# Hybrid diffusion step: the experts' shift added after the gather, router products in column tiles, last turns moved between dense products

## What is computed

```
h2 = rms(x, p['g_ffn']) * (1 + sc2) + sh2
aff = jax.nn.softmax((h @ w_router).astype(jnp.float32), axis=-1)
gate, idx = lax.top_k(jnp.swapaxes(aff, 1, 2), cap)
xg = jax.vmap(lambda hb, ib: hb[ib])(h, idx)
a = jnp.einsum('becd,edf->becf', xg, w_e1)
g3 = jnp.einsum('becd,edf->becf', xg, w_e3)
y = jnp.einsum('becf,efd->becd', jax.nn.silu(a) * g3, w_e2) * gate[..., None].astype(h.dtype)
```

## Time and profile before

| | us |
|---|---|
| median of 3 runs (3504.83 to 3505.77) | 3505.09 |
| the profiled execution | 3505.53 |
| its span | 3503.7 |
| PE busy | 3288.9 (94%) |
| DVE busy | 2107.6 (60%) |
| ACT busy | 1409.9 (40%) |
| POOL busy | 363.4 (10%) |

### The profile page before, as it was taken

The page is one execution under the profiler, slowest core; times in us unless marked ns, Lnnn a source line. Parts: engine busy times, 40 slices in busy tenths (PEclk is TensorE's granted clock), DMA queues, the critical chain, the costliest instruction groups (busy, mean ns, idle before and its releaser), DMA issues. The chain is left out here.

```text
span 3503.7 us, 39989 instructions
## 1 busy us (share of the span) xinstructions
PE 3288.9 (94%) x16088; PEld 2554.8 (73%) x16088; DVE 2107.6 (60%) x1830; ACT 1409.9 (40%) x1295; POOL 363.4 (10%) x429
## 2 busy tenths in 40 slices
PE   6889999999998899997999999939999999999995
PEld 4678878888886899986888888725666666666663
DVE  3336555555553677763232243257888888888886
ACT  3122212221211444442121222236777777777774
POOL 0020010010100000000011111030112111111102
PEclk8999999999999999999999999969999999999997
DMA  9465545465542211106253444168999999999996
GB/s 376 179 171 201 186 169 190 152 236 190 203 172 91 82 37 42 36 22 258 103 192 132 144 165 147 58 253 309 377 396 380 388 398 387 385 397 396 384 404 230
DMA packets 142462, 790.13 MB, mean 226 GB/s; under 512 B 18992, under 2 KB 30288, under 8 KB 61408
## 3 DMA queue, kind: packets, MB, share of 16 engines
q1 hardware_dynamic: 101680, 668.72, 49.6%
q0 software_dynamic: 40656, 119.60, 11.2%
HBM read 720.39 MB, written 67.86 MB: 225 GB/s over the span
## 5 line engine op out<-in xcount | busy, mean ns | idle before, releaser
L99 DVE TENSOR_TENSOR w_lo<-w_stage,w_hi 128x2048 fp32r<-128x2048 f32 x384 | 880.1, 2296 | 141.9 <-ACT w_hi L94 141.9
L94 ACT ACTIVATE w_hi<-w_stage 128x2048 fp32r<-128x2048 f32 x384 | 736.8, 1920 | 307.6 <-PE e_ps L106 307.5
L104 PE MATMUL i_ps<-w_hi,hT_hi 128*128 128x512 f32 (+1 forms) x1440 | 568.5, 395 | 25.0 <-DVE hT_lo L561 12.9
L105 PE MATMUL i_ps<-w_lo,hT_hi 128*128 128x512 f32 (+1 forms) x1440 | 559.2, 388 | 0.0
L106 PE MATMUL i_ps<-w_hi,hT_lo 128*128 128x512 f32 (+1 forms) x1440 | 558.9, 388 | 0.0
L104 PE MATMUL e_ps<-w_hi,xgT_hi 128*80 128x512 f32 x1024 | 404.3, 395 | 2.5 <-DVE xgT_lo L2038 2.3
L105 PE MATMUL e_ps<-w_lo,xgT_hi 128*80 128x512 f32 x1024 | 404.0, 395 | 0.0
L106 PE MATMUL e_ps<-w_hi,xgT_lo 128*80 128x512 f32 x1024 | 401.6, 392 | 0.0
L104 PE MATMUL p_ps<-w_hi,xT_hi 128*128 128x512 f32 x960 | 378.6, 394 | 17.8 <-DVE xT_lo L1534 17.8
L106 PE MATMUL p_ps<-w_hi,xT_lo 128*128 128x512 f32 x960 | 374.9, 391 | 0.0
L105 PE MATMUL p_ps<-w_lo,xT_hi 128*128 128x512 f32 x960 | 374.6, 390 | 0.0
(11 more groups left out here) (322 smaller groups left out, 4438.2 us busy)
## 6 DMA issues: line engine op xcount, KB each, us to landing
w_stage<-in_w_e SPq DMA_DIRECT2D x384, 1024.0 KB, 8.5
w_stage<-in_w_ada SPq DMA_DIRECT2D x96, 1024.0 KB, 6.4
w_raw<-in_w_in SPq DMA_DIRECT2D x64, 1024.0 KB, 4.8
w_stage<-in_w_o_gm SPq DMA_DIRECT2D x16, 1024.0 KB, 7.5
w_stage<-in_w_o_mla SPq DMA_DIRECT2D x16, 1024.0 KB, 5.1
w_stage<-in_w_out SPq DMA_DIRECT2D x16, 1024.0 KB, 4.8
acts<-evacuated POOLq DMA_DIRECT2D x60, 256.0 KB, 4.4
side<-acts POOLq DMA_DIRECT2D x40, 256.0 KB, 5.5
```

Of the source, the lines that this page charges most:

```text
L94: act.activation(dst, src, ACT.Copy).then_inc(st.hi, 1)
L99: dve.tensor_tensor(dst, src, hi.bitcast(F32), ALU.subtract).then_inc(st.split, 1)
L104: pe.matmul(out, x_hi, w_hi, start=first, stop=False)
L105: pe.matmul(out, x_hi, w_lo, start=False, stop=False)
```

## The change

1. The router's weights lie in `M.c_st` (16 tiles of 32 columns, 16 of them written anew). Each of the four products of `route` goes to a column tile of its own (output partitions 32j to 32j+31, each with start and stop), so `logitT` has 128 partitions, and the four parts are added only in the router: `logitT` is turned in five 128x128 tiles, and two reductions add the four groups.
2. The last chunk's turns 0 to 2 and products 0 and 1 stand between and behind the last dense tiles of the last piece.
3. POOL no longer waits for the stores of `xn` at the end of the phase; SP waits for them before the eighth piece of experts' weights, and POOL before the first gather.
4. The rows go to `h2` scaled, without the shift, from 5 buffers. The shift is loaded as 32 rows of 128, turned on PE, and laid out by DVE as `shiftT` (128x16x80). DVE adds it to the turned rows (`rows_sum`, three more instructions per expert, reading PSUM, writing `x_sum`), ACT rounds from `x_sum`, DVE subtracts from `x_sum`.
5. In the loop ACT rounds the thirds at steps 17 and 21 (16 and 20 before). DVE adds at steps 16 and 20, and subtracts at steps 18 and 22 (16 and 20 before).
6. `load_x(0)` stands ahead of the last gather.

The diff, cut to what the text speaks of:

```diff
-    w_r = m.new("w_router_sb", [P, KT, EXPERTS], F32)
+    w_r = M.c_st
...
-    M.logitT = m.new("logitT", [EXPERTS, N_TOK], F32)
+    M.logitT = m.new("logitT", [P, N_TOK], F32)
...
+        M.xn_stored = stored
...
-                    sp.dma_start(w_r[:], I["w_router"][0].rearrange("(k p) n -> p k n", p=P)).then_inc(w_r_in, 16)
+                    sp.dma_start(w_r[:, :, 0:EXPERTS], I["w_router"][0].rearrange("(k p) n -> p k n", p=P)).then_inc(w_r_in, 16)
...
-            for t in range(TT):
-                pool.wait_ge(stored[t], 16 * 2 * N_CH)
...
-                for a, b, src in ((0, P, ps[6][0:EXPERTS, 0:P]), (P, N_TOK, ps[7][0:EXPERTS, :])):
+                for a, b, src in ((0, P, ps[6][:, 0:P]), (P, N_TOK, ps[7][:])):
...
-                out = ps[7][0:EXPERTS, bass.ts(t - 1, P)] if t else ps[6][0:EXPERTS, 0:P]
+                out = ps[7][:, bass.ts(t - 1, P)] if t else ps[6][:, 0:P]
                 for j in range(KG):
-                    ins = pe.matmul(out, w_r[:, KG * i + j, :], x[:, j, :], start=(j == 0), stop=(j == KG - 1))
+                    ins = pe.matmul(out[32 * j:32 * j + 32, :], w_r[:, KG * i + j, :], x[:, j, :], start=True, stop=True, skip_group_check=True)
                 ins.then_inc(logit, 1)
...
+                    if n == N_PIECES - 1 and t >= 2:
+                        turn_xg(N_CH - 1, t - 2)
+                        if t >= 3:
+                            route(N_CH - 1, t - 3)
                 if c == chunk(OUT, 0) and g == 3:
                     sum_shift()
-            for t in range(TT):
+            for t in (3, 4):
                 turn_xg(N_CH - 1, t)
-                if t:
-                    route(N_CH - 1, t - 1)
+                route(N_CH - 1, t - 1)
             route(N_CH - 1, TT - 1)
...
-    h_row = [m.new(f"h_row{b}", [P, D], F32) for b in range(3)]
-    shift = m.new("shift2_rows", [P, 2, D], F32)
+    h_row = [m.new(f"h_row{t}", [P, D], F32) for t in range(TT)]
...
+    x_sum = m.new("x_sum", [P, KT, SLOTS], F32)
...
+    shiftT = m.new("shift2T", [P, KT, SLOTS], F32)
+    shift_rows = m.new("shift2_rows", [2 * KT, P], F32)
+    shift_cols = m.new("shift2_by_tile", [P, 2, KT], F32)
...
+        h_out = M.pool_sem("r_h_out")
...
-                sp.dma_start(shift[:, r, :], M.mod[r:r + 1, 3 * D:4 * D].to_broadcast((P, D))).then_inc(shift_in, 16)
+                sp.dma_start(shift_rows[bass.ts(r, KT), :], M.mod[r, 3 * D:4 * D].rearrange("(k p) -> k p", p=P)).then_inc(shift_in, 16)
             for q in range(PB):
+                if q == PB - 1:
+                    for t in range(TT):
+                        sp.wait_ge(M.xn_stored[t], 16 * 2 * (D // NC))
                 load(q, q, E13[0][0, q])
...
-            pool.wait_ge(shift_in, 32)
             for t in range(TT):
                 pool.wait_ge(scaled, 4 * t + 4)
-                pool.tensor_tensor(h_row[t % 3][:], h_row[t % 3][:], shift[:, min(t, 1), :], ALU.add).then_inc(h_ok, 1)
-                pool.wait_ge(h_ok, t + 1)
-                pool.dma_start(M.h2[bass.ts(t, P), :], h_row[t % 3][:]).then_inc(h_out[t % 3], 16)
-            for b in range(3):
-                pool.wait_ge(h_out[b], 32 if b < 2 else 16)
+                pool.dma_start(M.h2[bass.ts(t, P), :], h_row[t][:]).then_inc(h_out, 16)
+            for t in range(TT):
+                pool.wait_ge(M.xn_stored[t], 16 * 2 * (D // NC))
+            pool.wait_ge(h_out, 16 * TT)
             pool.wait_ge(pick_ok, 2)
             gather(0)
             gather(1)
...
+            load_x(0)
...
-            for t in range(N_F):
+            for t in range(1, N_F):
                 load_x(t)
...
             def rows_hi(e, g):
-                act.wait_ge(x_tr, 3 * e + g + 4)
-                dst, src = turned_rows(e, g, True)
-                act.activation(dst, src, ACT.Copy).then_inc(x_hi, 1)
+                act.wait_ge(x_ok, 3 * e + g + 1)
+                a, b = TXG[g]
+                act.activation(xT_hi[:, a:b, :], x_sum[:, a:b, :], ACT.Copy).then_inc(x_hi, 1)
...
-                    if j == 16 and rows:
+                    if j == 17 and rows:
                         rows_hi(i + 2, 0)
                         rows_hi(i + 2, 1)
-                    if j == 20 and rows:
+                    if j == 21 and rows:
                         rows_hi(i + 2, 2)
 
             def scale_rows(t):
-                if t >= 3:
-                    act.wait_ge(h_out[t % 3], 16)
                 for i in range(4):
-                    act.activation(h_row[t % 3][:, bass.ts(i, NC)].rearrange("p (j n) -> p j n", j=KG), M.xg[i][t], ACT.Copy,
+                    act.activation(h_row[t][:, bass.ts(i, NC)].rearrange("p (j n) -> p j n", j=KG), M.xg[i][t], ACT.Copy,
                                    scale=st[:, 3, t:t + 1]).then_inc(scaled, 1)
 
...
+            def rows_sum(e, g):
+                if g == 0 and not (isinstance(e, int) and e == 0):
+                    dve.wait_ge(x_lo, 3 * e)
+                dve.wait_ge(x_tr, 3 * e + g + 4)
+                a, b = TXG[g]
+                dve.tensor_tensor(x_sum[:, a:b, :], pair[0][:, g % 2, 0:(b - a) * SLOTS].rearrange("p (k n) -> p k n", n=SLOTS),
+                                  shiftT[:, a:b, :], ALU.add).then_inc(x_ok, 1)
+
             def rows_lo(e, g):
                 dve.wait_ge(x_hi, 3 * e + g + 1)
-                dst, src = turned_rows(e, g, False)
-                sub(dst, src, turned_rows(e, g, True)[0]).then_inc(x_lo, 1)
+                a, b = TXG[g]
+                sub(xT_lo[:, a:b, :], x_sum[:, a:b, :], xT_hi[:, a:b, :]).then_inc(x_lo, 1)
...
                     if j == 16 and rows:
+                        rows_sum(i + 2, 0)
+                        rows_sum(i + 2, 1)
+                    if j == 18 and rows:
                         rows_lo(i + 2, 0)
                         rows_lo(i + 2, 1)
                     if j == 19:
                         out(i, 0, n0 + 2 * PB + 4)
                     if j == 20 and rows:
+                        rows_sum(i + 2, 2)
+                    if j == 22 and rows:
                         rows_lo(i + 2, 2)
                     if j == 23:
                         out(i, 1, n0 + 2 * PB + 8)
...
+            by_group = lambda ap, n: ap[:, 0:n * P].rearrange("p (t j e) -> p t e j", t=n, j=KG)[:, :, 0:EXPERTS, :]
+            dve.tensor_reduce(logits[:, 0:4, :], by_group(pair[1][:, 0, :], 4), AX.X, ALU.add).then_inc(log_sum, 1)
+            dve.tensor_reduce(logits[:, 4:5, :], by_group(pair[1][:, 1, :], 1), AX.X, ALU.add).then_inc(log_sum, 1)
+            dve.wait_ge(log_sum, 2)
             for t in range(TT):
-                dve.scalar_tensor_tensor(logits[:, t, :], pair[1][:, 0, bass.ts(t, EXPERTS)], st[:, 3, t:t + 1], M.shift_logit[:, min(t, 1), :],
+                dve.scalar_tensor_tensor(logits[:, t, :], logits[:, t, :], st[:, 3, t:t + 1], M.shift_logit[:, min(t, 1), :],
...
+            dve.wait_ge(shift_tr, 1)
+            dve.tensor_copy(shift_cols[:].rearrange("p r k -> p (r k)"), pair[3][:, 1, 0:2 * KT]).then_inc(shift_col, 1)
+            dve.wait_ge(shift_col, 1)
+            for a, b, r in ((0, CAP_LAT, 1), (CAP_LAT, SLOTS, 0)):
+                dve.tensor_copy(shiftT[:, :, a:b], shift_cols[:, r, :].rearrange("p (k n) -> p k n", n=1).to_broadcast((P, KT, b - a))).then_inc(shift_ok, 1)
...
-            for g in range(3):
-                rows_lo(0, g)
+            dve.wait_ge(shift_ok, 2)
+            rows_sum(0, 0)
+            rows_sum(0, 1)
+            rows_lo(0, 0)
+            rows_sum(0, 2)
+            rows_lo(0, 1)
+            rows_lo(0, 2)
             for j in range(N0):
                 lo(j + LEAD, j + LEAD, None)
             hidden(0)
             dve.wait_ge(gate_in, 32)
-            for g in range(3):
-                rows_lo(1, g)
+            rows_sum(1, 0)
+            rows_sum(1, 1)
+            rows_lo(1, 0)
+            rows_sum(1, 2)
+            rows_lo(1, 1)
+            rows_lo(1, 2)
...
                 if g == 2:
-                    pe.wait_ge(x_lo, 3 * e + 1)
+                    pe.wait_ge(x_ok, 3 * e + 1)
...
-                ins = pe.transpose(pair[1][:, 0, bass.ts(t, EXPERTS)], M.logitT[:, bass.ts(t, P)], M.ident[0:EXPERTS, 0:EXPERTS])
+                ins = pe.transpose(pair[1][:, t // 4, bass.ts(t % 4, P)], M.logitT[:, bass.ts(t, P)], M.ident[:])
             ins.then_inc(log_tr, 1)
+            pe.wait_ge(shift_in, 32)
+            pe.transpose(pair[3][:, 1, 0:2 * KT], shift_rows[:], M.ident[0:2 * KT, 0:2 * KT]).then_inc(shift_tr, 1)
```

More of the change, by code:

```diff
@@ L1767, in phase_experts @@
     gate2 = m.new("gate2", [SLOTS, D], F32)
+    x_sum = m.new("x_sum", [P, KT, SLOTS], F32)
+    assert m.at <= M.phase_at + 2 * X_END + X_END // 2
+    m = Map(nc, M.phase_at + X_END + X_END // 4 + 3 * 4 * PIECE)
+    shiftT = m.new("shift2T", [P, KT, SLOTS], F32)
+    shift_rows = m.new("shift2_rows", [2 * KT, P], F32)
+    shift_cols = m.new("shift2_by_tile", [P, 2, KT], F32)
+    assert m.at <= M.phase_at + 2 * X_END
```

(8 more changed lines are left out.)

## The result

| | before | change |
|---|---|---|
| median, us | 3504.96 (3502.63 to 3505.77, 4 runs) | 3544.25 (3543.43 to 3545.41, 4 runs) |
| profiled execution / its span | 3505.53 / 3503.7 | 3544.59 / 3542.6 |
| ratio | | 1.0110 [1.0098, 1.0122] |
| POOL busy, us | 363.4 | 304.4 |
| DVE busy, us | 2107.6 | 2129.3 |

The change is 39 us slower. The forecast was 3534, the range 3510 to 3558. The two spans differ by 38.9 us, and three marks show where. DVE multiplies `hidden` once per expert; the first of these, the last, and the span's end stand at

The account below looks back on a forecast made before the run. PE was taken to bound the dense phase and experts' loop, a chain of waits the router between. Terms -6.0, -2.2, -8.7, +35, +14 and -3 gave +29 us on 3505.53, forecast 3534, range 3510 to 3558.

Parts of the forecast that it names:

- router groups in the dense stream: Dense phase: column tiles save 0.4 us per group in 15 groups on PE, -6.0 us (0 to -12).
- end of the dense phase: After the last dense product: 4.4 us in place of 7.9, against 1.7 laid ahead, -2.2 us (-1 to -3.5).
- router: Between dense phase and experts: without shift load and additions the first turn comes 10 us earlier, -8.7 us net (-12 to -4).
- loop, stall: Experts' loop: PE waits for the last third's rows, 2.5 us a pass in 14 passes, +35 us (+29 to +39).
- loop, clock: Experts' loop: PE's pauses may be followed by half clock, +14 us (0 to +30).
- end: Kernel's end: the first xn load, ahead of the last gather, starts about 3.5 us sooner, -3 us (0 to 5 gained).
- main step: Loop, step 22: last third is subtracted behind piece 25, so PE waits 2.2 us at the head of its body.
- (a): Loop: the stall is there but the clock stays up, 3520 us; chance 0.18.
- (b): Loop: clock falls after each pause, longer than 3.4 us, +30 instead of +14, 3550 up to 3560; chance 0.10.
- Rival (e): Router products: column tiles save nothing, +6 us, inside the range; chance 0.52 together with the forecast.
- Rival (c): Loop: PE does not wait, only the gains of -20 us are left, 3485 us; chance 0.12.
- (d): Whole kernel: larger gains, stall of 2.1 us and no lost clock, -3 us, 3503, no change; chance 0.08.

Follow-up runs that it names:

- third_first: The change with the last third subtracted ahead of piece 25 in step 22 instead of behind it; 3495.71 us, ratio 0.9974 to before.
- lo_17_21: The change with the thirds subtracted at steps 17 and 21 instead of 18 and 22; 3490.48 us, ratio 0.9957 to before.
- turns_late: `lo_17_21` with the last block's turns and router groups put back behind the last dense product; 3491.61 us.
- tiles_alone: The kernel before with only the router products in column tiles, their four parts added by DVE; 3496.39 us, ratio 0.9973.

## Why the prediction was right

| term | predicted | measured in the trace |
|---|---|---|
| router groups in the dense stream | -6.0 | -9.3 |
| end of the dense phase | -2.2 | -2.2 (4.5 - 8.1 + the 1.5 laid ahead) |
| router | -8.7 | -5.5 |
| loop, stall | +35 | +40.6 |
| loop, clock | +14 | +16 |
| end | -3 | -0.6 |
| sum | +29 | +39 (38.9 between the spans) |

**The main step** held: the last third stands on DVE behind piece 25, PE waits at the head of its body, in every pass, and nothing makes it up. `third_first` shows that this order makes 50.0 of the 56.8 us that the loop lost; of the rest, 4.7 is what `third_first` has over `lo_17_21`, and 2.1 what `lo_17_21` has over before. The wait itself was 2.6 us (I had 2.2, and 0.3 for what comes on top). The pass grew by 2.9. Where PE loses the other 0.3 us is not shown: no other wait of 0.1 us or more stands in the loop. That is the term whose size was most off, +5.6 us.

**The clock** held too, and between rivals (a) and (b). I took it from two pauses, one followed by the low clock and one not. Of the 14, 10 were, costing 1.2 to 1.5 us for a stretch of 3.4 and 2.8 for the one of 6.8. The rate could not have been read from two pauses: that "somewhat over half" of 24 us came within 2 us of the measured 16 is in good part luck. The trace of before has two more of this length that I did not use, 2.26 us until 1555.02 and 2.63 us until 1568.78; both came with the clock at 0.50, for 3.4 and 6.8 us.

**Column tiles**: I took a saving of 0.4 us per group, from 1.05 to about 0.6. Duration and spacing both fell by 0.62, about midway between my 0.4 and what only counting the columns gives (0.8). Rival (e) falls. This miss of 3.3 us and the router's of 3.2 have opposite signs and cancel, which is luck. So is it that the sum of the terms meets the spans' difference to 0.1 us, given the spread of 9 us named above. By Theoretical Speedup in TensorEngine Tiling (Array Packing), in the Trainium skill, a side of at most 32 gives up to four times; the trace shows 2.7 (0.98 to 0.36). The same page's Key Properties say that changing the mode drains the array. Here groups stand directly between dense products and turns at 0.36 us, so what a switch costs is inside that.

**Dense end**: the size is right, its working is not. I put nearly all of it on the turns that move. `turns_late` gives these 0.6 us, and `tiles_alone` gives 1.8 at the same place to the shorter groups, of which five stand behind the last dense product. ACT started 11.2 us earlier in all, and the two terms give 11.5, but a start in the span isn't known that well.

**Router**: the landing of the writes came where the sum had it, 34.4 us after the table load, predicted 2336.5 - 2302.5 = 34.0. The queues shared by halves, as in the earlier trace rows; from 2316 to 2324 us of the change:

```profile
q0 software_dynamic: 233, 1.78, 52.5%
q1 hardware_dynamic: 230, 1.66, 49.2%
```

The picks were there at 29.4 (I had 29.5). The text ahead of the prediction has the DMA engines at 90% and more in this hole; before, they were so only from 2320 to 2340 us (a share of 1.01), with 0.76 from 2298 to 2320 and 0.71 from 2340 to 2360. Too good was what follows. "Gather as before (8.2 us)" failed: it was 10.5. And POOL's copy, in no term of the sum, went from 0.18 to 1.33, because the writes now land while DVE is still subtracting. With the landing's 0.4 these two are the 4 us by which the first turn fell short: it came 5.9 us sooner after the table load, where I had 10. The additions gave back 0.9 us of that: they cost the first product 0.4, where I had 1.3 for both experts.

**End**: the first block's wait fell from 5.36 to 0.66 us, as predicted. But the piece behind it on ACT then waits for PE:

```profile
3482.24 1.03 ACT L2004 ACTIVATE e_ps<-f_x 128x1024 f32<-128x1024 f32 x1 [0.66 <-DMA f_x<-xn]
...
3487.99 1.92 ACT L94 ACTIVATE w_hi<-w_stage 128x2048 fp32r<-128x2048 f32 x1 [3.42 <-PE e_ps L106]
```

The step "pieces of weights stand behind it on ACT" was true, but those pieces wait for PE anyway. Of the term of 3 us, 0.6 came between these two traces; over all kernels it is not known better than 0.4 to 3.

Rival (c) is refuted for the change. It was a description of `lo_17_21`, though: the gains without the stall, 3485 forecast and 3490.5 measured. (d) is refuted by the 40.6 us of stall.

## What to carry to other kernels

Where an engine works a few pieces ahead and each piece is released by the bottleneck engine, a small operation queued behind such a piece inherits its release time. Put it ahead of the piece: two neighbouring lines swapped were worth 48 us here. When a pause on PE is costed, cost the clock behind it as well (here 40% on top of the stall). And when a chain is shortened, ask which work it now runs beside: the gather took 2.3 us longer than before, beside the weights, and POOL stood still for DVE.

## What was not expected of the hardware

- POOL made no headway beside DVE's subtractions of 128x2048: a copy of 80x1 numbers took 0.4 to 6.4 us and ended with them in nine kernels, and the issue of an indirect gather took 6.35 us in place of 0.98 in two. The Trainium skill has a rule for the copy, in SBUF — State Buffer, section SBUF: two separate sides: a GpSimd instruction that reads SBUF and a DVE instruction with two inputs from SBUF take a shared pair of ports in turn, each for a whole instruction. The runs agree, with one difference: POOL did not get in between the three subtractions (2.29 us each), but only behind the last. For the descriptors that POOL writes, the same section of the Trainium skill names only DVE instructions in a 2-port mode as what holds them up; here the issue of the gather ended 0.86 us behind plain subtractions with two inputs, so for this indirect gather the measurement goes further than the page.
- It goes the other way too. Three subtractions took 9.65 us before, when POOL's last addition ran beside them for 3.1 us, and 6.67 in the change, 3.0 less:

```profile
2335.01 9.65 DVE L99 TENSOR_TENSOR w_lo<-w_stage,w_hi 128x2048 fp32r<-128x2048 f32 x3 [1.25 <-ACT w_hi L94]
```
```profile
2320.75 6.67 DVE L99 TENSOR_TENSOR w_lo<-w_stage,w_hi 128x2048 fp32r<-128x2048 f32 x3
```

- The cast of 80 numbers fell from 1.91 to 0.19 us. Before, it ended at 2332.74, and the POOL addition that ran beside it at 2332.68.
- In the loop, pauses of PE of 0.2 us never came with the low clock, those of about 2.6 us in 10 of 14 passes, those of 4.9 us in all 14.
- Column-tiled groups of four fp32 products between turns: 0.36 us from start to start instead of 0.98.
